# First sparse layer: six projections on the undivided residual, and index products in four row strips between projections

## What is computed

```python
h = h + rms_norm(sq_relu_mlp(a, mlp_w1, mlp_w2), gain)      # end of mlp1
u = rms_norm_2(x, norm1_g) @ w_in                           # x is that h
dq, dk, dv, iq, ik, iw = ...                                # 16 heads of 64; one key, one value; 8 index heads of 32
idx = einsum('bqhd,bsd->bqhs', iqb, ik)                     # index products, contraction over 32
idx = einsum('bqh,bqhs->bqs', iwb, relu(idx))               # weighted sum over 8 heads
idx = where(key_pos <= t, idx, -inf)
_, sel = top_k(idx, 128)                                    # which keys a query may see
s = einsum('bqhd,bqkd->bqhk', qb, k_sel) * scale            # attention over those keys
```

## Time and profile before

| what | value |
|---|---|
| median of 3 runs | 2826.14 us (2822.95 to 2826.61) |
| profiled execution: own time, span | 2824.09 us, 2822.3 us |
| PE busy | 2685.0 us (95%) |
| DVE busy | 1627.2 us (58%) |
| ACT busy | 1142.3 us (40%) |
| PE in the chain that ended last | 79% |

### The profile page before, as it was taken

The page is one execution under the profiler, slowest core; times in us unless marked ns, Lnnn a source line. Parts: engine busy times, 40 slices in busy tenths (PEclk is TensorE's granted clock), DMA queues, the critical chain, the costliest instruction groups (busy, mean ns, idle before and its releaser), DMA issues.

```text
span 2822.3 us, 38838 instructions
## 1 busy us (share of the span) xinstructions
PE 2685.0 (95%) x13937; PEld 2153.7 (76%) x13937; DVE 1627.2 (58%) x3039; ACT 1142.3 (40%) x1982; POOL 117.6 (4%) x104
## 2 busy tenths in 40 slices
PE   7999999999999999998999998999999989999998
PEld 5567888887887888886866875677777768788887
DVE  6335825557786725545854267755677775563451
ACT  4444322236774322224355317832455552322221
POOL 0000000000000000000320010000011110000000
PEclk9999999999999999998999989999999999999999
DMA  4112333322222333321211310022222212423331
GB/s 142 45 60 60 112 98 96 98 74 76 78 77 68 97 100 94 99 88 45 75 46 31 105 45 2 1 75 82 83 68 68 75 53 90 134 90 100 94 99 65
DMA packets 59684, 217.82 MB, mean 77 GB/s; under 512 B 6432, under 2 KB 6560, under 8 KB 59424
## 3 DMA queue, kind: packets, MB, share of 16 engines
q1 hardware_dynamic: 57920, 209.76, 24.3%
q0 software_dynamic: 1632, 6.29, 0.6%
HBM read 211.83 MB, written 4.19 MB: 77 GB/s over the span
## 4 chain that ended last, share of the span: by engine, by line
PE 79%; DVE 11%; ACT 3%; DVEq 3%; issue 3%; ACTq 0%; DMA 0%; POOL 0%; SPq 0%
PE ps L379 23%; PE ps L380 22%; PE ps L381 22%; DVE work L2328 1%; PE ps L520 1%; DVE ring_lo L319 1%; DVE big L3487 1%; DVEq L3545 1%; PE ps L771 1%; DVE work L2347 1%; PE ps L2253 1%; PE ps L2489 1%; ACT ring_hi L312 1%; PE ps L2082 1%; PE ps L581 1%
## 5 line engine op out<-in xcount | busy, mean ns | idle before, releaser
L379 PE MATMUL ps<-a_hi,ring_hi 128*128 128x512 f32 (+1 forms) x1960 | 775.6, 396 | 39.2 <-DVE ring_lo L319 23.8
L381 PE MATMUL ps<-a_hi,ring_lo 128*128 128x512 f32 (+1 forms) x1976 | 765.7, 387 | 0.0
L380 PE MATMUL ps<-a_lo,ring_hi 128*128 128x512 f32 (+1 forms) x1896 | 735.0, 388 | 0.0
L319 DVE TENSOR_TENSOR ring_lo<-ring,ring_hi 128x1024 fp32r<-128x1024 f32 x358 | 438.1, 1225 | 503.5 <-ACT ring_hi L312 474.4
L312 ACT ACTIVATE ring_hi<-ring 128x1024 fp32r<-128x1024 f32 x376 | 395.7, 1055 | 500.0 <-PE ps L381 499.5
L379 PEld LDWEIGHTS ps<-a_hi,ring_hi 128*128 128x128 f32 x1960 | 373.1, 190 | 124.9 <-DVE ring_lo L319 17.9
L381 PEld LDWEIGHTS ps<-a_hi,ring_lo 128*128 128x128 f32 x1976 | 376.0, 190 | 76.0
L380 PEld LDWEIGHTS ps<-a_lo,ring_hi 128*128 128x128 f32 x1896 | 360.7, 190 | 70.2 <-issue 1.2
L380 PE MATMUL ps<-hid_lo,ring_hi 128*128 128x512 f32 (+1 forms) x992 | 380.3, 383 | 0.0
L379 PE MATMUL ps<-hid_hi,ring_hi 128*128 128x512 f32 (+1 forms) x928 | 354.6, 382 | 0.0
L381 PE MATMUL ps<-hid_hi,ring_lo 128*128 128x512 f32 (+1 forms) x928 | 354.2, 382 | 0.0
(11 more groups left out here) (444 smaller groups left out, 3231.2 us busy)
## 6 DMA issues: line engine op xcount, KB each, us to landing
ring<-weights SPq DMA_DIRECT2D x392, 512.0 KB, 3.6
h<-x SPq DMA_DIRECT2D x1, 2048.0 KB, 9.2
residual<-h POOLq DMA_DIRECT2D x4, 512.0 KB, 3.4
h<-residual POOLq DMA_DIRECT2D x1, 2048.0 KB, 11.0
out<-h POOLq DMA_DIRECT2D x1, 2048.0 KB, 7.9
tab<-tables SPq DMA_DIRECT2D x1, 1648.0 KB, 15.5
big<-positions SPq DMA_DIRECT2D x1, 256.0 KB, 3.8
col<-columns SPq DMA_DIRECT2D x1, 164.5 KB, 4.0
```

Of the source, the lines that this page charges most:

```text
L319: dve.tensor_tensor(lo, M.ring[:, b % RING, :], hi.bitcast(F32), ALU.subtract).then_inc(M.sem("blocks_split"), 1)
L379: pe.matmul(out, w_hi, hi, start=start, stop=False)
L380: pe.matmul(out, w_hi, lo, start=False, stop=False)
L381: return pe.matmul(out, w_lo, hi, start=False, stop=stop)
```

## The change

1. The passage from mlp1 to dsa takes the `open_halves` form: 4 blocks by token halves on the undivided residual (`open_hi`, `open_lo`, over parts of the hidden tiles that are free), then projections 4 and 5 on it at full width in banks 4 and 5. The branch norm's second half is totalled and spread between the down and open products. Two weight roundings go behind ACT's tiles 3 and 5 of the second half. Block slots and holders change to suit.
2. The norm's factor is spread inside projection 4 (`factor`). DVE multiplies output tiles 3, 0, 4 and 5 by it (`times_factor`); the index queries stay undivided (a positive factor per query row doesn't change an order), the index weights get it per token on ACT. DVE and ACT then form the divided, split input at full width (`scale`, `high`, `low`) for projections 6 to 19.
3. The index key is copied to four row strips (`R.ik`) without zeros. `index(n)` issues 4 products, each contracting over 32 rows in its own strip, into banks 2 to 5: once after projection 6, then in the middle of and after projections 7 and 8, and in the middle of 9. ACT has 4 relu buffers; the sum is kept in bank 6.
4. Head totals move to projections 10 to 18, the root behind the last projection's output on ACT, all 9 spreads behind projection 19.
5. In hgrn two semaphores are merged into one (`hg_sig_log`); order and waits stay the same.

```diff
         self.dsa_y_lo = at("dsa_y_lo", 4096 + 24 * T, NT, T, dt=F32R)
+        self.open_hi = at("open_hi", 4096 + 24 * T, NT, T, dt=F32R)
+        self.open_lo = at("open_lo", 4096 + 9 * T, NT, T, dt=F32R)
         self.first_hi = at("first_hi", 4096 + 28 * T, BLK * P, dt=F32R)
         self.first_lo = at("first_lo", 4096 + 30 * T, BLK * P, dt=F32R)
         self.a2_lo = at("a2_lo", 35328, NT, T, dt=F32R)
...
 HOLDER = {FIRST["hgrn_heads"] + 3: FIRST["hgrn_heads"] - 2, FIRST["hgrn_heads"] + 6: FIRST["hgrn_heads"] + 3}
+HOLDER.update({FIRST["dsa_in"] + t: FIRST["dsa_in"] + t - 6 for t in range(2, 8)})
...
     if b == FIRST["hgrn_heads"] + 3:
         slot = (b - 1) % RING
         return M.ring_hi[:, slot, :], M.ring_lo[:, slot, :], RING
+    if FIRST["dsa_in"] + 2 <= b < FIRST["dsa_in"] + 6:
+        slot = (b - 6) % RING
+        return M.ring_hi[:, slot, :], M.ring_lo[:, slot, :], 2
     if b < FIRST["dsa_in"] or b >= FIRST["ff_up0"]:
...
-        holder = SPLIT_BLOCKS[splits_before(b) - 2] if slots == 2 else HOLDER.get(b, b - slots)
+        holder = HOLDER.get(b, SPLIT_BLOCKS[splits_before(b) - 2] if slots == 2 else b - slots)
...
-def open_halves_pe(pe, M, norm, name, n, a_lo, branch):
+def open_halves_pe(pe, M, mlp, norm, name, n, hi, lo, branch):
...
         round_block(act, M, first + n, fresh=(name == "mlp1"))
-    if name == "mlp0":
-        round_block(act, M, first + 2, fresh=True)
+    round_block(act, M, first + 2, fresh=(name == "mlp0"))
     half_square_act(act, M, name, 0)
     half_branch_root_act(act, M, name, 0)
-    if name == "mlp0":
-        round_block(act, M, first + 3)
-        return
-    half_square_act(act, M, name, 1)
-    half_branch_root_act(act, M, name, 1)
+    round_block(act, M, first + 3)
...
-        self.relu = b[:, 15:17, :]
-        self.ikz = b[:, 17:21, :]
+        self.kv, self.scale = b[:, 4, :], b[:, 22, :]
+        self.ik, self.relu = b[:, 17, :], b[:, 18:22, :]
         p, at = [], 0
         for _ in range(4):
             v, at = M.carve(at, 1280)
         self.staged, at = M.carve(at, 4, T)
         self.iw, at = M.carve(at, QT, 8)
         self.best, at = M.carve(at, 8)
...
         self.pairs = Pairs(M, "dsa", 4, self.q, self.view, self.staged,
                            [(self.key, self.value, lambda half: self.mask)], self.y, 0)
...
+OPEN_TILES = 6
+FIRST_TOTAL = 10
+def dsa_pe(pe, M, R, branch_last):
     used, free = M.sem("blocks_used"), M.sem("dsa_in_free")
...
+    def project(t, bank, hi, lo, between={}, wait=None):
         b = FIRST["dsa_in"] + t
         wait_split(pe, M, b)
         for k in range(BLK):
...
+            if k in between:
+                between[k]()
+            if wait:
+                wait(k)
+            mm = split_matmul(pe, M, M.bank(bank), b, k, hi[:, k, :], lo[:, k, :], k == 0, k == 7)
         mm.then_inc(used, 1)
...
+    def factor():
+        pe.wait_ge(M.sem("norm_inverse"), 1 + M.past("norm_4", "inverse"))
+        norm_spread_pe(pe, M, M.norm_bank("norm_4"), lambda c: R.scale_col[:, c:c + 1].broadcast_to([P, P]))\
+            .then_inc(M.sem("norm_spread"), 1)
+    def turn(bank, src):
         for t in range(QT):
...
+            mm = pe.transpose(M.bank(bank)[:, t * P:(t + 1) * P], src[:, t * P:(t + 1) * P], M.t("ident", P))
+        return mm
+    def index(n):
+        i, g = 1 + n // 2, n % 2
+        if n:
+            pe.wait_ge(M.sem("dsa_relu"), 4 * n)
+        for j in range(4):
+            rows = slice(32 * j, 32 * j + 32)
+            pe.matmul(M.bank(2 + j)[:, 0:S_LEN[i]], R.iq[rows, g, i * P:(i + 1) * P], R.ik[rows, 0:S_LEN[i]],
+                      start=True, stop=True).then_inc(M.sem("dsa_index"), 1)
+    open_halves_pe(pe, M, "mlp1", "norm_4", "dsa_in", 4, M.open_hi, M.open_lo, branch_last)
+    project(4, 4, M.open_hi, M.open_lo, {1: factor})
+    project(5, 5, M.open_hi, M.open_lo)
+    pe.wait_ge(free, 2)
     pe.wait_ge(M.sem("small_kept"), 1)
...
+    pe.wait_ge(M.sem("dsa_scaled"), 2)
+    turn(2, R.value_t)
+    turn(3, R.narrow).then_inc(M.sem("turned_in"), 1)
+    pe_scaled = M.past("norm_4", "scaled") + 2 * NT
+    project(6, 0, M.a_hi, M.a2_lo, wait=lambda k: pe.wait_ge(M.sem("norm_scaled"), pe_scaled + k + 1))
+    pe.wait_ge(M.sem("small_done"), 3)
+    pe.wait_ge(M.sem("small_kept"), 2)
+    pe.wait_ge(M.sem("dsa_scaled"), 4)
+    index(0)
+    for t in range(7, 12 + NT):
+        pe.wait_ge(free, t - 5 if t > 7 else 1)
+        project(t, t % 2, M.a_hi, M.a2_lo, {4: lambda: index(2 * t - 13)} if t < 10 else {})
+        if t < 9:
+            index(2 * t - 12)
+        if FIRST_TOTAL <= t < FIRST_TOTAL + 9:
+            head_total_pe(pe, M, "dsa_norm", t - FIRST_TOTAL)
     def spread(k):
         if k == 0:
             pe.wait_ge(M.sem("norm_inverse"), 1 + M.past("dsa_norm", "inverse"))
             pe.wait_ge(M.sem("norm_scaled"), k - 1 + M.past("dsa_norm", "scaled"))
         head_spread_pe(pe, M, k)
...
+    for k in range(9):
         spread(k)
...
+    pe.wait_ge(free, 2 + 6 + NT)
     R.pairs.pe(pe, M)
 def dsa_act(act, M, R):
+    given = M.sem("dsa_in_free")
+    def done(t):
+        act.wait_ge(M.sem("blocks_used"), FIRST["dsa_in"] + t + 1)
     def out(t):
...
+        done(t)
+        if t < 12:
+            act.activation(R.q[:, t - 4, :], M.bank(t % 2), ACT.Copy).then_inc(given, 1)
         else:
...
+            act.activation(M.m[:, t - 12, :], M.bank(t % 2), ACT.Sigmoid).then_inc(given, 1)
         round_block(act, M, FIRST["dsa_in"] + t + 2)
...
+    def high(k):
+        act.wait_ge(M.sem("tile_scaled"), k + 1)
+        act.activation(M.a_hi[:, k, :], M.sq[:, k % 2, :], ACT.Copy).then_inc(M.sem("tile_rounded"), 1)
+    def both(dst, rows):
+        for to in HALVES:
+            act.activation(dst[to, :], R.kv[rows, :], ACT.Copy)
+    def keys(js):
+        for j in js:
+            act.activation(R.ik[32 * j:32 * j + 32, :], R.narrow[0:32, :], ACT.Copy)
+    for t in (1, 2):
+        done(t)
+        act.activation(R.iq[:, t - 1, :], M.bank(t), ACT.Copy).then_inc(given, 1)
+    norm_act_root(act, M, "norm_4", D)
+    for t in (6, 7):
+        round_block(act, M, FIRST["dsa_in"] + t)
+    act.wait_ge(M.sem("dsa_scaled"), 2)
+    both(R.value_t, UPPER)
+    act.drain().then_inc(M.sem("small_kept"), 1)
+    for k in range(4):
+        high(k)
+    keys(range(2))
+    for k in range(4, 6):
+        high(k)
+    keys(range(2, 4))
+    act.drain().then_inc(M.sem("small_kept"), 1)
+    for k in range(6, NT):
+        high(k)
+    both(R.key, LOWER)
     act.wait_ge(M.sem("turned_in"), 1)
     act.activation(R.value, M.bank(2), ACT.Copy)
...
+    for t in range(QT):
+        act.activation(R.iw[:, t, :], M.bank(3)[:, t * P + 32:t * P + 40], ACT.Copy, scale=R.scale_col[:, t:t + 1])
     act.drain().then_inc(M.sem("small_done"), 1)
...
+    def relu(n):
+        i = 1 + n // 2
+        for j in range(4):
+            act.wait_ge(M.sem("dsa_index"), 4 * n + j + 1)
+            if n:
+                act.wait_ge(M.sem("dsa_weighted"), 4 * (n - 1) + j + 1)
+            act.activation(R.relu[:, j, 0:S_LEN[i]], M.bank(2 + j)[:, 0:S_LEN[i]], ACT.Relu)\
                .then_inc(M.sem("dsa_relu"), 1)
...
+    def square(k):
         if k >= 2:
             act.wait_ge(M.sem("norm_summed"), k - 1 + M.past("dsa_norm", "summed"))
         act.drain()
...
+        act.activation(M.sq[:, k % 2, :], R.q[:, k - 1, :] if k else R.key, ACT.Square).then_inc(M.sem("norm_squared"), 1)
+    act.wait_ge(M.sem("norm_scaled"), 3 * NT + M.past("norm_4", "scaled"))
+    for t in range(6, 12 + NT):
         out(t)
...
+        if t < 9:
+            relu(2 * t - 12)
+            relu(2 * t - 11)
+        if FIRST_TOTAL - 1 <= t < FIRST_TOTAL + 8:
+            square(t - FIRST_TOTAL + 1)
+    act.wait_ge(M.sem("norm_summed"), 9 + M.past("dsa_norm", "summed"))
+    act.activation(M.root[:, 0:72], M.bank(7)[:, 0:72], ACT.Sqrt, bias=M.eps, scale=1.0 / 64)\
+       .then_inc(M.sem("norm_root"), 1)
     R.pairs.act(act, M)
...
+def dsa_dve(dve, M, R):
+    gain = lambda k: M.c("norm1", k)
+    rest_block(dve, M, FIRST["dsa_in"] + 4)
+    dve.wait_ge(M.sem("norm_root"), 1 + M.past("norm_4", "root"))
+    dve.reciprocal(R.scale_col, M.root[:, 0:QT]).then_inc(M.sem("norm_inverse"), 1)
+    dve.wait_ge(M.sem("norm_spread"), 1 + M.past("norm_4", "spread"))
+    dve.tensor_copy(R.scale, M.norm_bank("norm_4"))
+    dve.drain()
+    def times_factor(t, dst, bank):
+        dve.wait_ge(M.sem("blocks_used"), FIRST["dsa_in"] + t + 1)
+        dve.tensor_tensor(dst, M.bank(bank), R.scale, ALU.mult).then_inc(M.sem("dsa_scaled"), 1)
+    def scale(k):
+        dve.scalar_tensor_tensor(out=M.sq[:, k % 2, :], in0=M.h[:, k, :], scalar=gain(k), in1=M.norm_bank("norm_4"),
+                                 op0=ALU.mult, op1=ALU.mult).then_inc(M.sem("tile_scaled"), 1)
+    def low(k):
+        for half in range(2):
+            dve.wait_ge(M.sem(f"residual_out{2 * half + k // 4}"), 16)
```

(42 more changed lines are left out.)

311 lines of the change are left out of this document (38 added, 273 removed), and 2 rows, old and new, of the table NORMS.

## The result

The changed kernel takes 2802.53 us, median of 4 runs (2798.44 to 2804.15), against 2826.14; the ratio is 0.9918, 95% interval [0.9905, 0.9931]. That is 23.6 us less. The forecast was 2792.5, so the direction is right and 10 us of a forecast gain of 33.5 are missing. The profiled execution took 2803.71 us, its span is 2801.9.

The account below looks back on a forecast made before the run. PE was taken as the bound, with time to win only where it idles, is slow or waits. The first attention mask moves from 1446.76 to 1410.6, 36.2 won, less 2.7 for clock, net 33.5: 2792.5 us, range 2786 to 2804.

Parts of the forecast that it names:

- Open products: Mlp1-to-dsa passage: four open tiles end 44.46 us after the last down tile's first half-width product, as in hgrn's passage.
- Index products: Six index calls around projections 7 to 9: 6.5 us in all, where one block took 17.9; first call 0.8.
- What is late next: Behind projection 19: top-k ends 1397.8, its reciprocal lets head spreads start at 1398.5, PE idles 3.9 us, mask 1410.6.
- POOL's 2.41 for block 5 and DVE's 1.22 for blocks 4 and 6 lie a projection ahead of need: Before projection 6: these low-part additions would not be late, so projection 6 would not wait for its low part.
- Top-k ends 65.05 later: DVE's top-k, started at 1332.7, would keep its earlier length of 65.05 us and end at 1397.8.
- The low clock: After PE's idle time behind projection 19: 5.4 us at half rate, charged as 2.7 us.
- what follows it is the same work: Everything behind the first attention mask was taken as unchanged, so the mask's time was the point to predict.
- Strips in a row: Rival: index strips don't overlap, costing 17.9 + 1.2 for 6.5, all behind 11 us later: 2804; chance 0.08.
- Calls wait: Rival: index calls 1, 3, 5 each find ACT 1.5 us behind, or DVE slower with PSUM sums: 4.5 later, 2797; chance 0.17.
- Top-k isn't the bound: Rival: stall behind projection 19 shrinks to ACT's way, 3.1 us, and the clock holds: 2789; chance 0.10.
- slower: Rival: PE drops to 1.2 GHz in the half-width stage and stays there, about 2853 us; chance 0.03.
- nothing changes: Rival: mask stays at 1446.8, DVE's weighted sums ending 34 us later behind calls waiting 5.6 us each; chance 0.01.

Follow-up runs that it names:

- the edit that bears on it: Changed kernel with block 6's low part added by POOL in place of DVE, POOL's blocks 5 to 7 in a row: 2797.52 us, ratio 0.9905.
- one row strip: Changed kernel with all four products of each index call reading rows 0 to 31, so index values are wrong: 2809.6 us, ratio 0.9947.
- the two POOL edits: Changed kernel with POOL's blocks 8 to 10 held until the first weighted sums, and POOL adding block 6 for DVE; with 16 idle products 2795.78 us.
- The kernel with three edits: Changed kernel with POOL's blocks 8 to 10 delayed, block 6 moved to POOL, and 16 idle products before the head spreads: 2795.78 us, ratio 0.9899.

## Why the prediction was right in sign and 10 us off

**Open products: right.** +44.7 against +44.46, clock 1.00 throughout, and projection 19 ends at +152.7 (1408.66 - 7.98 - 1248.00), forecast +150.7, all of the difference being ahead of the first index call. No low clock came ahead of 1390 (1.00 from 1248 to 1407) and PE waited at none of calls 1 to 5.

**Index products: right.** From projection 7's start at 1315.60 to projection 10's at 1337.66 is 22.06 us with five calls; forecast 16.3 + 5.7 = 22.0. The first call took 0.65 to projection 7 (0.8 forecast), so the six are 6.4 in all. Taking hgrn's strips as the nearest row held (6.5); the estimate of 7.4 that stood beside it was 1 too high. The 17.9 us charged for the old block is its length at full clock; it took 18.9 in the profile on record. What the forecast did not see is that the strips are worth nothing in one block: their gain and that of the place go together.

**What is late next: the top-k, right, but too early.** Its reciprocal, not ACT, ended PE's idle time, and cutting the top-k's rounds moved the stretch. The step that failed is "POOL's 2.41 for block 5 and DVE's 1.22 for blocks 4 and 6 lie a projection ahead of need", with the durations "8 subtractions (0.69)", "weighted sums of 512 columns take about 0.81 each" and "Top-k ends 65.05 later". I asked of each queue when its result is needed, and not what POOL's rests do to the DVE instructions that they lie beside. All three terms were mis-sized by it:

- the low part 2.27 for 0.69: first index call at +66.95 for +65.0, 2.0 late, 1.6 of it this
- first weighted sum of 512 columns 2.45: last call to top-k 6.91 for 5.0, of which 1.6 goes away with POOL's rest
- the `TENSOR_SCALAR` behind the first tile 2.47 for 0.29: top-k 67.3 for 65.05, 2.2

Together 5.4 to 6.1 us. The low clock gave 0.9 back (1.8 for 2.7), which leaves 4.5 to 5.2 of the 5.1 missing in the stretch. The second term was removed by an edit; the first is read from its row, as the edit that bears on it changed two things; the third was put to the test by no edit, but the top-k without such a collision took 65.1 us (one row strip). With the two POOL edits the top-k starts at +89.01, forecast +88.8, and the reciprocal comes at +155.39, forecast +153.9, as one `TENSOR_SCALAR` still took 1.25 for 0.36. The trace of before held the hint, in two rows of DVE's timeline:

```profile
1358.44 0.29 DVE L2600 TENSOR_SCALAR work<-work 128x256 f32<-128x256 f32 x1
...
1379.93 0.60 DVE L2600 TENSOR_SCALAR work<-work 128x384 f32<-128x384 f32 x1
```

The one of 384 columns took longer than that of 512 in the earlier trace rows; one of POOL's rests, at 1377.91 for 2.41, ran beside its start. I read 65.05 as a fixed length, though its collisions move with the phase of two queues.

**Outside the stretch: not in the forecast.** I made the sum against one execution of before. Its stretch was 202.87, the mean of three profiles is 202.0; 2.6 are lost behind the mask and 0.7 ahead of it. So 202.0 - 174.9 = 27.1 won in the stretch (means of three and two profiles), less 3.3, is 23.8, beside 23.6 and 24.4 measured. The sum closes, but of the 3.3 the 0.7 is well within the spread (1243.7 to 1248.2), and the cause of the 2.6 stays open. The step that failed here is "what follows it is the same work": the instructions are the same, their time was put at the same without a reason.

**The rivals.** "Strips in a row" is refuted. "Calls wait" gave DVE slower where the sum lives in PSUM as one of its ways: its price, 4.5, is near the truth, by luck: its mechanism isn't, as it is the operands still in SBUF that stall, and PE waited at none of calls 1 to 5. "Top-k isn't the bound", "slower" and "nothing changes" are refuted.

**A better version.** The kernel with three edits has a stretch 5.3 us shorter than the mean of the changed kernel's two, and 2795.78 us; its ratio 0.9899 [0.9882, 0.9916] overlaps 0.9916 [0.9903, 0.993], so by time alone it isn't proved better; what shows the gain is the stretch.

## What to carry to other kernels

Moving work earlier changes what it lies beside: for each moved DVE instruction with two operands in SBUF, and for each `TENSOR_SCALAR` on SBUF, list POOL's instructions in the same us and put the rest of POOL's instruction on top in the bound. A short block of small products is worth little faster if two other engines pace it; laid in the gaps of long work it is nearly free. And when an end point has three feeders (here top-k, root, PE), price all three before adding filler work: 16 idle products (6.8 us) took longer than the 5.3 us gap that was left once the top-k came earlier.

## What the runs showed of the hardware

- A DVE instruction with two SBUF operands stood still for up to the whole of a POOL `TENSOR_TENSOR` of 2.40 us: 0.68 became 2.27, 0.49 became 2.39, and a `TENSOR_SCALAR` of 256 columns, 0.29, became 2.47. `MAX8` and sums with one operand in PSUM did not, nor did a `TENSOR_SCALAR` that started 0.27 us ahead of POOL's instruction (0.29).
- Four row-strip products between full-array projections cost 0.65 to 1.07 us a call, entering, leaving and an increment on each included; with all four in one strip 1.92 to 4.33 us.
- With PE busy 10.99 of 19.92 us the granted clock was 0.55, so that most of it was at the lower of the two levels (1.2 GHz); and it was 0.87 in a window in which PE was busy 10.00 of 10.00 us. Behind an idle time of 3.81 us the next 9.5 to 11.1 us were granted 1.00 in one execution and 0.85 in another.
